# Taking the q, k and v projections with the weights as the stationary side

## The reference, cut to what matters

```python
h = rmsnorm(x, g_pre[i])
proj = h @ w_in[i]                                   # 2048 x 20512 weights
qkv, z_a, b_raw, a_raw, glu_in, z_b, gate_logits = jnp.split(proj, ...)
qkv = jax.nn.silu(causal_depthwise_conv(qkv, w_conv_qkv[i]))     # 4 taps along the tokens
q, k, v = jnp.split(qkv, 3, axis=-1)
q, k, v = l2norm(heads(q)), l2norm(heads(k)), heads(v)           # 16 heads of 128
o_a = gated_delta_chunked(q, k, v, g_log, beta)                  # chunks of 64 tokens
o_a = rmsnorm(o_a, g_dn_out[i]) * jax.nn.silu(z_a)
...
u = causal_depthwise_conv(glu(glu_in), w_dw[i]) + b_dw[i]        # the other branch, 31 taps
u = jax.nn.silu(layernorm(u, ln_g[i], ln_b[i])) * jax.nn.silu(z_b)
```

## Time and profile before

| what | us |
|---|---|
| median of three runs | 2548.47 (2547.51 to 2551.29) |
| the profiled execution | 2548.92 |
| its span | 2547.4 |
| PE busy | 2461.4 (97%) |
| DVE busy | 1629.1 (64%) |
| ACT busy | 1155.0 (45%) |
| POOL busy | 175.4 (7%) |

### The profile page before, as it was taken

One profiled execution on the slowest core, in us unless ns is written; L12 is line 12 of the kernel. 1 busy time (PEld: TensorE's weight loads), 2 busy tenths in 40 slices (PEclk: granted clock), 3 DMA queues, 4 the chain that ended last, 5 costly groups with the idle time before them and its releaser, 6 DMA issues.

```text
span 2547.4 us, 34830 instructions
## 1 busy us (share of the span) xinstructions
PE 2461.4 (97%) x13453; PEld 2046.6 (80%) x13453; DVE 1629.1 (64%) x2146; ACT 1155.0 (45%) x1475; POOL 175.4 (7%) x254
## 2 busy tenths in 40 slices
PE   7999999988999999999999889999999999999997
PEld 6878878867888888788887778888888888888886
DVE  5899999678585766646546655656465544565554
ACT  5444444455353535334445454444444444443443
POOL 3000000153000101001000010000000000000000
PEclk9999999989999999999999999999999999999999
DMA  7566666445343344648655445655565655675563
GB/s 233 187 203 205 211 202 205 156 158 166 117 149 117 133 133 142 212 161 276 235 185 187 165 155 175 207 168 203 171 204 163 224 187 193 205 274 192 188 218 113
DMA packets 226899, 469.75 MB, mean 184 GB/s; under 512 B 12217, under 2 KB 13090, under 8 KB 225634
## 3 DMA queue, kind: packets, MB, share of 16 engines
q1 hardware_dynamic: 214018, 418.57, 49.5%
q0 software_dynamic: 12768, 49.59, 5.6%
HBM read 445.05 MB, written 23.07 MB: 184 GB/s over the span
## 4 chain that ended last, share of the span: by engine, by line
PE 70%; DVE 3%; ACT 2%; issue 1%; POOL 0%; DVEq 0%; ACTq 0%; POOLq 0%
PE acc L2119 60%; PE aux L2265 3%; PE aux L2149 1%; PE aux L2351 1%; PE aux L2355 1%; DVE w_lo L1376 1%; DVE cy L1632 0%; PE aux L2276 0%; ACT w_hi L809 0%; PE aux L2340 0%; PE aux L2350 0%; PE aux L2535 0%; PE aux L2534 0%; PE acc L2442 0%; ACT qT L1053 0%
## 5 line engine op out<-in xcount | busy, mean ns | idle before, releaser
L1376 DVE TENSOR_TENSOR w_lo<-raw,w_hi 128x1024 fp32r<-128x1024 f32 x790 | 973.0, 1235 | 817.1 <-ACT w_hi L809 805.6
L809 ACT CAST w_hi<-raw 128x1024 fp32r<-128x1024 f32 x790 | 827.0, 1051 | 1188.3 <-PE acc L2119 1176.0
L2119 PE MATMUL acc<-w_hi,r1h 128*128 128x512 f32 (+1 forms) x1920 | 764.1, 398 | 7.4 <-DVE r1l L1461 4.4
L2119 PE MATMUL acc<-w_lo,r1h 128*128 128x512 f32 (+1 forms) x1920 | 747.5, 389 | 0.0
L2119 PE MATMUL acc<-w_hi,r1l 128*128 128x512 f32 (+1 forms) x1920 | 747.4, 389 | 0.0
L2119 PE MATMUL acc<-w_hi,r2h 128*128 128x512 f32 x1216 | 477.5, 393 | 2.2 <-DVE w_lo L1376 1.9
L2119 PE MATMUL acc<-w_lo,r2h 128*128 128x512 f32 x1216 | 473.5, 389 | 0.0
L2119 PE MATMUL acc<-w_hi,r2l 128*128 128x512 f32 x1216 | 473.5, 389 | 0.0
L2119 PEld LDWEIGHTS acc<-w_hi,r1h 128*128 128x128 f32 x1920 | 362.6, 189 | 85.8 <-issue 5.1
L2119 PEld LDWEIGHTS acc<-w_hi,r1l 128*128 128x128 f32 x1920 | 362.1, 189 | 76.1
L2119 PEld LDWEIGHTS acc<-w_lo,r1h 128*128 128x128 f32 x1920 | 362.6, 189 | 69.9 <-issue 1.0
(11 more groups left out here) (442 smaller groups left out, 1591.3 us busy)
## 6 DMA issues: line engine op xcount, KB each, us to landing
raw<-in_w_in SPq DMA_DIRECT2D x264, 1024.0 KB, 5.0
raw<-in_w_out SPq DMA_DIRECT2D x32, 1024.0 KB, 4.9
raw<-in_w_br_b SPq DMA_DIRECT2D x16, 1024.0 KB, 4.9
raw<-in_w_br_a SPq DMA_DIRECT2D x16, 1024.0 KB, 5.3
raw<-in_w_ple_gate SPq DMA_DIRECT2D x16, 1024.0 KB, 4.9
raw<-in_w_o_mla SPq DMA_DIRECT2D x16, 1024.0 KB, 4.9
raw<-in_w_o_conv SPq DMA_DIRECT2D x16, 1024.0 KB, 4.9
raw<-in_w_q_b SPq DMA_DIRECT2D x8, 1024.0 KB, 5.1
```

The lines of the kernel that those rows point to most:

```text
L809: nc.scalar.copy(w_hi[:, h % HL, 0:n], raw[:, k % RAW, x * HALF:x * HALF + n]).then_inc(hi_ready, 1)
L1376: V.tensor_tensor(w_lo[:, h % HL, 0:n], raw[:, k % RAW, x * HALF:x * HALF + n], w_hi[:, h % HL, 0:n].bitcast(F32), ALU.subtract).then_inc( ...
L2119: ins = T.matmul(acc[:, s, x, 0:n], a[:, kt0 + k, xs_], w[:, h % HL, at], start=start and k == 0 and m == 0, stop=stop and k == kts - 1 an ...
```

## The change

For blocks 0 to 2 of every pass the sides are exchanged: a new function takes 128x128 of the weights as the stationary side and streams the 256 tokens, so that the block's sum comes out as channels by tokens. A half is then 24 matmuls of 128x256. Block 3 and all other phases stay with `gemm`. With that the eight transposes of `praw` and one of the two rounds of ACT copies go, and `cpad` is filled straight from `acc`. The table `OWN` is drawn together: the convolution starts a slot or two earlier and takes four slots, four steps in each, for every n, and for k and v what follows it comes a slot earlier. The scaling of k goes from slot 31 to 30, and PE's slot 0 waits for one semaphore more. Some semaphores are merged.

```diff
-OWN = ((8, 9, 10, (11, 14), 15, 16), (16, 18, 19, (20, 22), 23, 24), (24, 25, 26, (27, 29), 30, 31))
-OWN_BANKS = (2, 2, 0)
+OWN = ((8, (10, 13), 14, 16), (16, (18, 21), 22, 23), (24, (25, 28), 29, 30))
 # ACT, own
                     if hl == evac:
-                        if n or not first:
-                            act.wait_ge(sem("ch_tr"), i * 3 + n)
                         act.wait_ge(w_used, used(ph, 8 * n + 7, i))
-                        for x in range(TT):
-                            nc.scalar.copy(praw[:, x], acc[:, n % 2, x]).then_inc(acc_free[n % 2], 1)
-                    if hl == pad:
-                        act.wait_ge(sem("ch_tr"), i * 3 + (n + 1))
                         act.wait_ge(sem("conv4_done"), i * 3 + (n + 1))
-                        b = OWN_BANKS[n]
-                        c.inc(nc.scalar.copy(cpad[:, 0:2, SHORT - 1:], X[:, b].rearrange("p (a b) -> p a b", a=2)))
-                        sig(nc.scalar.copy(cpad[:, 2:4, SHORT - 1:], X[:, b + 1].rearrange("p (a b) -> p a b", a=2)),
-                            "cpad_ready", i * 3 + (n + 1))
+                        for q in range(2):
+                            nc.scalar.copy(cpad[:, 2 * q:2 * q + 2, SHORT - 1:],
+                                           acc[:, n % 2, q].rearrange("p (a b) -> p a b", a=2)).then_inc(acc_free[n % 2], 1)
 # DVE, own
                     if hl == conv:
-                        dve.wait_ge(sem("cpad_ready"), i * 3 + (n + 1))
+                        dve.wait_ge(acc_free[n % 2], freed(ph, n, i))
-                if hl == 31:
+                if hl == 30:
                     dve.wait_ge(sem("cols_ready"), i + 1)
 # PE
+            def channel_half(ph, hl, i, ops):
+                bl, q = divmod(hl, 8)
+                h, b = ph.h0 + hl, ph.b0 + bl
+                s = b % 2
+                pe.wait_ge(lo_ready, LO_CREDIT + h + 1 + i * ph.hn)
+                if q == 0:
+                    pe.wait_ge(acc_free[s], 2 * (b // 2) + i * ph.bn)
+                for k in range(2):
+                    for a in range(CT):
+                        at = slice(k * NB + a * P, k * NB + (a + 1) * P)
+                        for m, (r, w) in enumerate(((ops[0], w_hi), (ops[1], w_hi), (ops[0], w_lo))):
+                            ins = T.matmul(acc[:, s, a // 2, a % 2 * TOK:(a % 2 + 1) * TOK], w[:, h % HL, at], r[:, 2 * q + k],
+                                           start=q == 0 and k == 0 and m == 0 and a % 2 == 0, stop=q == 7 and k == 1 and m == 2 and a % 2 == 1)
+                ins.then_inc(w_used, 1)
+
+            def heads_half(ph, hl, i, ops):
+                if hl < 8 * 3:
+                    channel_half(ph, hl, i, ops)
+                else:
+                    model_half(ph, hl, i, ops)
 # PE, own
-                    if hl == to_channels:
-                        pe.wait_ge(acc_free[n % 2], freed(ph, n, i))
-                        if n == 1:
-                            pe.wait_ge(sem("tok_ready"), i * 2 + 1)
-                        channels_first(cols(praw), OWN_BANKS[n]).then_inc(sem("ch_tr"), 1)
 # PE, delta
                 if hl == 0:
+                    if dv(2, 0):
+                        pe.wait_ge(sem("oT_lo"), dv(2, 0))
                     pe.wait_ge(sem("kb_ready"), dv(1, 1))
 # PE, the four passes
-                model_half(ph, hl, 0, r1)
+                heads_half(ph, hl, 0, r1)
```

More of the change, by code:

```diff
@@ L103 @@
 TR_GAINS, TR_NARROW, TR_ROWS = range(1, 4)
+SMALL_DECAYS, SMALL_MEAN, SMALL_RSTD, SMALL_P = range(1, 5)
 ROW_SLOT = P // KT
@@ L317, in build_layer @@
             s1 = lambda n, shape, dt=F32: sb(n, shape, dt, st)
-            praw = s1("praw", [P, TT, NB])
+            s1("pad_own", [P, TT, NB])
             cpad = s1("cpad", [P, GH, SHORT - 1 + TOK])
@@ L977, in own @@
             def own(ph, hl, i, first):
-                for n, (evac, _, pad, (_, conv_end), silu, back) in enumerate(OWN):
+                for n, (evac, (conv, conv_end), silu, back) in enumerate(OWN):
                     if hl == back + 1 and n < 2:
@@ L1620, in own @@
                         c.link(V.tensor_copy(wq4[:, n], pc[:, bass.ds(i * GH, GH), R_SC + n:N_ROWS:3]))
-                for n, (_, _, _, (conv, conv_end), silu, back) in enumerate(OWN):
+                for n, (_, (conv, conv_end), silu, back) in enumerate(OWN):
                     if hl == conv:
-                        dve.wait_ge(sem("cpad_ready"), i * 3 + (n + 1))
+                        dve.wait_ge(acc_free[n % 2], freed(ph, n, i))
                     if conv <= hl <= conv_end:
@@ L2244, in own @@
             def own(ph, hl, i):
[L2245 to L2250 removed]
+                for n, (_, _, _, back) in enumerate(OWN):
                     if hl == back:
@@ L2318, in delta @@
                         if l < LEVELS - 1:
-                            if hl == 10 and i is not None:
-                                pe.wait_ge(sem("cpad_ready"), i * 3 + 1)
                             ins = per_chunk(2, rows_of(uinv), rows_of(xs))
@@ L2388, in _ @@
                 for hl in range(ph.hn):
[L2389 removed]
+                    heads_half(ph, hl, i, r1)
                     if hl == 9:
```

20 lines of the change are left out of this document (9 added, 11 removed).

## The result

The changed kernel takes 2552.98 us (median of 12 runs, 2551.25 to 2555.81), the kernel before beside it 2548.05 (12 runs, 2547.06 to 2551.29): a ratio of 1.0021, 95% interval 1.0013 to 1.0029. The profiled execution took 2551.99 us, of which 2550.5 are its span; that of before took 2548.92 with 2547.4. By the spans of the two traces the change thus costs 3.1 us, by the medians 4.9.

What follows compares the result with a forecast made beforehand. The prediction took PE to bound passes 1 to 3, but to wait in pass 0. Its terms, 14.4 - 10.5 - 2.9 + 2.9 = +3.9 us, gave 2552 us (+0.14%), own range 2547 to 2558, overall range 2543 to 2562.

Steps and rivals of the forecast that it cites:

- The halves: PE, 96 halves in four passes: 24 narrow matmuls take 2.87 us in place of 2.72, +14.4 us in all.
- The bounds of 0 and 29: Limits on the halves' cost: 0 if narrow matmuls become as good as wide, 96 x 0.3 if the second load is twice as dear.
- The transposes: PE: twelve groups of eight transposes of `praw` go, 0.87 us each, -10.5 us in all.
- Waits in passes 1 to 3: PE: k's wait goes, shorter waits for gating and `cth` come; -0.95 us a pass, -2.9 in all.
- The -0.3 of slot 8: Slot 8 of passes 1 to 3: a short PE wait that longer halves cover, -0.3 us a pass.
- Waits in pass 0: PE waits in pass 0: +2.9 us, the pass as a whole longer by 3.4 to 4.4, taken as 3.9.
- The leg by leg account: Pass 0 followed along DVE's list in three legs, from q's convolution at 543.3 to k's transposes at 615.0 to 616.0.
- The first wait: Pass 0: PE's wait for `cth` of q, forecast at 5.3 us instead of 10.77.
- The second: Pass 0: PE's wait for `cth` of k, in slot 23 instead of 24, forecast at 6 us or more.
- A: Pass 0 gains, the layer norm's chain not being lengthened: about -9 instead of +2.9, total -8, 2540.5 us; chance 0.20.
- B: DVE and ACT fall behind in slots 25 to 30 of passes 1 to 3: +12, 2564 us; chance 0.18.
- C: Narrow matmuls cost next to nothing in the exchanged order: -11.5 from the sum, 2541 us; chance 0.03.

Runs made afterwards that it cites:

- slots_old: The changed kernel with the old slots of convolution, tanh and transposes back, and the k products at slot 31: 2549.73 us, ratio 1.0005 against the kernel before.
- port_free: The changed kernel with DVE's layer norm product, and so POOL's and `luh`, one slot later for q and k: 2553.92 us, 1.0023 against the kernel before.
- pass0_old: The changed kernel with the old slots of the convolution and what follows it in pass 0 alone: 2547.72 us, ratio 0.9996 against the kernel before.

## Why the prediction was right

The forecast was 2552.0 us and no change that can be told; 2552.98 came, 4.9 us over before against 3.9 forecast. The mechanism was the one argued: PE's own work about level, a loss in pass 0 that the other passes don't have. That the sum came so close is in part luck. By stage, pass 0 was forecast at +3.9 and measures +5.0; the three others were forecast level (three times +1.0 of work and -0.95 of waits) and measure -1.1. The two misses cancel. By its terms:

- **The halves**, +14.4 forecast. Measured 4 x 2.43 = +9.7. This is the term that was mis-sized most. The pitch was right (120 ns, 2.87 us), but I took halves with a like neighbour ahead, and in the passes they stand between transposes, where the difference is 0.10 to 0.12. The bounds of 0 and 29 held it.
- **The transposes**, -10.5 forecast. Measured 4 x 2.11 = -8.4 by the period, as a price of PE's work; in pass 0, where PE waits anyway, only 0.9 of it comes out. The durations were right, what I missed is a cover that goes with them, the 0.4 us in front of `xs`. The two errors partly cancel: +3.9 forecast for both; the two kernels that do one each give +1.3, and slots_old, which does both, +1.0 over the four passes.
- **Waits in passes 1 to 3**, -0.95 a pass forecast. The single waits came as worked out: 1.36 for `qT` (1.4 forecast), 0.46 for `cth` (0.45), nothing for k (under 0.3), 0.20 at most for `ol`. The -0.3 of slot 8, for which the forecast shows no row, isn't there in full: from one group of the solve to the next that slot takes 4.20 us in pass 2 before and after, 0.17 more than its neighbours before (4.03) and 0.05 more after (4.15), and a later slot waits 0.20 for `xs`. With it the waits fell by 0.6 a pass and not 0.95. Against slots_old the slots gave -0.4 a pass. The pass has 137.90, 0.3 less than the 138.2 forecast, since its halves are cheaper.
- **Waits in pass 0**, +2.9 forecast. Measured 5.0 - 1.0 = +4.0. The leg by leg account held within 1 us, mostly on the late side: q's convolution ended at 542.96 (543.3 forecast), k's `cth` at 579.97 (579.5 at best), the last layer norm product at 592.91 (592.3 to 593.1), the last `lul` at 602.57 (601 to 602), the k product started at 613.10 (612.4 to 613.4), k's transposes at 616.15 (615.0 to 616.0). Since the pass began 0.48 earlier than in the trace on which the forecast counted, 0.5 has to be added to each: then the last `lul` is the one furthest off, 1.0 behind its range. The first wait was 6.99 in place of 5.3: PE was there 0.8 earlier (0.5 of it by the start of the pass), and `cth` ended 1.1 later. The second was 7.49, in slot 23 (6 or more). Pass 0 came out at +5.0; I had taken 3.9 of 3.4 to 4.4. Against the exchange alone the new slots cost 4.0 there.
- **Rivals.** A (pass 0 gains) fell at the place named: the last `lul` ended at 602.6, not 597.5. B (the gating slips in passes 1 to 3) fell: the wait in slot 29 is 1.36. C fell: the halves cost 0.10 each.

So the change loses by where it puts q's, k's and v's slots in the one pass that PE doesn't bound. The exchange itself is worth nothing here, since 10 us of narrower matmuls and 8 us of transposes are nearly a trade at par.

That POOL's product would block `cth` stood in the forecast as up to 3.3 us, and 2.1 came, twice. The Trainium skill, "SBUF — State Buffer", section "Who interferes with whom", says that a VectorE instruction with both inputs in SBUF and a GpSimd instruction that reads SBUF exclude one another, whoever starts first, to the end of that instruction. The trace agrees: `cth` ends 1.07 us behind POOL's end in q's leg and 579.97 - 578.89 = 1.08 in k's, and the `w_lo` of 2.72 us ends 561.65 - 560.56 = 1.09 behind the second product. The page's rule tells where the block is, but not what it is worth: port_free took it away and the kernel became no faster.

No version here that does all the work beats the kernel before by more than can be measured. The nearest is pass0_old, 0.9996 (0.9987 to 1.0005).
